# One decoder block on one core: GpSimd adds up the two parts of h, bucket copies split, small reorderings at the start and before the output projection

## The reference, cut to what matters

```python
def reference(x, attn_norm_g, w_in, ...):          # 512 tokens, 1024 channels, float32
    h = rmsnorm(x, attn_norm_g[l])
    proj = h @ w_in[l]
    u_b, u_c, u_x, q, k, v, g_conv, g_attn = jnp.split(proj, SPLITS, axis=-1)
    y_conv = (u_b * short_conv(u_c * u_x, conv_w[l])) @ w_conv_out[l]
    attn = sliding_window_attention(q, k, v, attn_sinks[l], rel_bias)   # 16 heads, 2 KV heads, window 128
    mixed = sigmoid(g_conv) * y_conv + sigmoid(g_attn) * (attn @ w_attn_out[l])
    x = x + mixed @ w_o[l]
    h2 = rmsnorm(x, mlp_norm_g[l])
    x = x + square(relu(h2 @ w_up[l])) @ w_down[l]
    return rmsnorm(x, final_norm_g)
```

## Time and profile before

| | |
|---|---|
| time, median of 3 runs | 752.34 us (752.04 to 752.34) |
| the profiled execution's own time | 752.0 us |
| its span in the trace | 750.3 us |
| PE busy | 740.4 us (99%), 4201 matmuls |
| DVE busy | 656.4 us (87%) |
| ACT busy | 429.7 us (57%) |
| POOL busy | 85.2 us (11%) |
| DMA | 135.45 MB, mean 181 GB/s |
| granted PE clock | 0.9 or more in all 40 slices |

### The profile page before, as it was taken

One profiled execution on the slowest core, in us unless ns is written; L12 is line 12 of the kernel. 1 busy time (PEld: TensorE's weight loads), 2 busy tenths in 40 slices (PEclk: granted clock), 3 DMA queues, 4 the chain that ended last, 5 costly groups with the idle time before them and its releaser, 6 DMA issues.

```text
span 750.3 us, 10666 instructions
## 1 busy us (share of the span) xinstructions
PE 740.4 (99%) x4201; PEld 650.1 (87%) x4201; DVE 656.4 (87%) x759; ACT 429.7 (57%) x548; POOL 85.2 (11%) x120
## 2 busy tenths in 40 slices
PE   8999999999999999999999999999999999999996
PEld 8899888888888888888878899889988999899985
DVE  6995888889899686989999999998799879986997
ACT  6773555453644557564658776654465455545555
POOL 1520000111122101010100101010101010100102
PEclk9999999999999999999999999999999999999999
DMA  9999313162247987778766747777677668676703
GB/s 324 188 309 333 113 56 114 57 159 66 84 125 232 310 232 193 199 224 200 248 169 168 217 125 209 181 196 197 169 186 203 176 170 220 168 212 182 196 0 114
DMA packets 69443, 135.45 MB, mean 181 GB/s; under 512 B 2636, under 2 KB 18068, under 8 KB 69396
## 3 DMA queue, kind: packets, MB, share of 16 engines
q1 hardware_dynamic: 48848, 85.23, 33.9%
q0 software_dynamic: 20336, 49.30, 30.6%
q10 hardware_dynamic: 212, 0.28, 0.1%
HBM read 128.48 MB, written 6.32 MB: 180 GB/s over the span
## 4 chain that ended last, share of the span: by engine, by line
PE 94%; DMA 3%; DVE 1%; ACT 1%; issue 0%; DVEq 0%; ACTq 0%
PE pair L1086 45%; PE pair L1045 21%; PE pair L790 6%; PE pair L792 6%; PE pair L791 6%; PE pair L912 4%; DMA q_raw<-in_w_in 3%; PE pair L837 2%; PE pair L812 1%; PE pair L811 1%; PE pair L821 1%; PE pair L1008 0%; DMA xn<-in_x 0%; PE pair L996 0%; PE pair L851 0%
## 5 line engine op out<-in xcount | busy, mean ns | idle before, releaser
L1386 ACT ACTIVATE high<-home_raw 128x2048 fp32r<-128x2048 f32 x91 | 174.4, 1916 | 148.8 <-PE pair L1086 103.4
L2005 DVE TENSOR_TENSOR home_lo<-home_raw,high 128x2048 fp32r<-128x2048 f32 x91 | 208.4, 2291 | 34.0 <-ACT high L1386 33.6
L1086 PE MATMUL pair<-high,s_hi_tile 128*128 128x512 f32 x440 | 110.3, 391 | 0.7 <-ACT pair L1571 0.7
L1086 PE MATMUL pair<-high,s_lo_tile 128*128 128x512 f32 x440 | 109.9, 390 | 0.0
L1086 PE MATMUL pair<-home_lo,s_hi_tile 128*128 128x512 f32 x440 | 109.5, 389 | 0.0
L1086 PEld LDWEIGHTS pair<-high,s_hi_tile 128*128 128x128 f32 x440 | 81.8, 188 | 18.1 <-issue 1.1
L1086 PEld LDWEIGHTS pair<-home_lo,s_hi_tile 128*128 128x128 f32 x440 | 82.5, 188 | 17.1
L1086 PEld LDWEIGHTS pair<-high,s_lo_tile 128*128 128x128 f32 x440 | 82.5, 188 | 17.0
L790 PE MATMUL pair<-h,wgt 128*128 128x512 f32 x192 | 76.5, 399 | 0.0
L792 PE MATMUL pair<-h,wgt 128*128 128x512 f32 x192 | 75.0, 390 | 0.0
L791 PE MATMUL pair<-h,wgt 128*128 128x512 f32 x192 | 74.9, 390 | 0.0
(11 more groups left out here) (227 smaller groups left out, 1127.5 us busy)
## 6 DMA issues: line engine op xcount, KB each, us to landing
home_raw<-in_w_up SPq DMA_DIRECT2D x16, 1024.0 KB, 5.4
home_raw<-in_w_down SPq DMA_DIRECT2D x16, 1024.0 KB, 5.0
raw<-in_w_in SPq DMA_DIRECT2D x26, 512.0 KB, 4.8
home_raw<-in_w_up POOLq DMA_DIRECT2D x12, 1024.0 KB, 8.3
home_raw<-in_w_down POOLq DMA_DIRECT2D x12, 1024.0 KB, 8.5
home_raw<-in_w_in POOLq DMA_DIRECT2D x7, 1024.0 KB, 8.6
home_raw<-in_w_in SPq DMA_DIRECT2D x7, 1024.0 KB, 6.7
home_raw<-in_w_conv_out SPq DMA_DIRECT2D x4, 1024.0 KB, 5.2
```

Source lines behind the costliest of these rows:

```text
L1086: last = mm(pair[region(s, i)][:, b, :], a_[:, k, b * P:(b + 1) * P], w[:, k, :], start=(fresh and kind == 0 and k == 0), stop=(kind == 2 ...
L1386: a(high[n % 2][:, :], home_raw[home_of(s, name)][:, :], ACT.Copy).then_inc(m_hi, 1)
L2005: v.tensor_tensor(home_lo[home][:, :], home_raw[home][:, :], f32(high[n % 2][:, :]), ALU.subtract).then_inc(m_lo, 1)
```

## The change

POOL adds high and low part of the first token half of h into a new tile `h_whole`, in two instructions of 128 x 1024 elements (`first_whole`): the first between `add_q(M7)` and the bucket copies, the second between `add_q(M5)` and the first store. The three sums of h that use the first token half then take DVE one operation each. Of the 32 bucket copies, 14 stay where they were and 18 move behind `add_q(N4)`. `h_s1` moves ahead of `q_sum_t2`. ACT writes the second token half so that the first four tiles are whole before the last two are begun. The high parts of M1's weights are made in quarters, those of M5's in halves (and M5's kind 0 goes by k). At the start, the gains are transposed and copied before the second block of x is waited for, and 3 idle transposes fewer are made. In stage WO the first half of the seed copy stands before `s_high(WO, N2)`.

```diff
-        hs_part = place("hs_part", [P, 4, 2 * P], offset=hs_at[0])
+        h_whole = place("h_whole", [P, KT, 2 * P], offset=one[3])
...
+            def first_whole(j):
+                u = h_whole[:, 4 * j:4 * j + 4, :]
+                g.tensor_tensor(u, f32(four_of(h[:, 0, :, :], 0, j)), f32(four_of(h[:, 1, :, :], 0, j)), ALU.add
+                                ).then_inc(h_added, 1)
+            def buckets(first, end):
...
             add_q(M7, 1, 1, q_t3_in)
+            pool.wait_ge(h_ready, 8)
+            first_whole(0)
             pool.wait_ge(table_in, 16 * 2)
             pool.wait_ge(ext_step, 1)
...
+            buckets(0, 14)
...
+            first_whole(1)
             store_sum(M6)
             pool.wait_ge(q_low, 5)
             add_q(N4, 1, 0, q_t4_in)
+            buckets(14, BUCKETS)
             store_sum(M5)
...
-            idle_transposes(28)
-            x_transposes(0)
+            idle_transposes(25)
             pe.wait_ge(rows_in, 16 * 3)
             nc.tensor.transpose(bank[KT - 1][:, T - 5 * KT:T], prow[:, :], ident[0:5 * KT, 0:5 * KT]).then_inc(par_t, 1)
+            x_transposes(0)
             x_transposes(1)
...
-                        by_k = i == M6 and kind == 0
+                        by_k = i in (M6, M5) and kind == 0
...
+                n = 512 if i == M1 else 1024
+                for c0 in range(1024 * e, 1024 * e + 1024, n):
+                    a(q_hi[Q_ORDER.index(i) % 2][:, cols(c0, n)], q_raw[i][:, cols(c0, n)], ACT.Copy).then_inc(q_high, 1)
+
+            def q_high_t1(e):
+
+                act.wait_ge(q_t1_in, 16)
+                act.wait_ge(q_prod, 2 * Q_ORDER.index(N2) + 2)
                 c = cols(1024 * e, 1024)
-                a(q_hi[Q_ORDER.index(i) % 2][:, c], q_raw[i][:, c], ACT.Copy).then_inc(q_high, 1)
+                a(q_hi[1][:, c], q_raw[M5][:, c], ACT.Copy).then_inc(q_high, 1)
...
+            tile_whole(0, 0)
+            tile_whole(1, 4)
...
+            for k in (1, 5, 2, 3, 6, 7):
+                tile_whole(LATE_TILES.index(k), k)
...
             sum_high(M6)
+            sum_high(M5)
             q_high_t2()
-            sum_high(M5)
-            q_high_part(M5)
+            q_high_t1(0)
+            q_high_t1(1)
...
+            seed_out(0)
             s_high(WO, N2)
...
+            seed_out(1)
...
             scale_x(0)
-            scale_x(1)
             dve.wait_ge(par_t, 1)
             v.tensor_copy(pcol[:, :], bank[KT - 1][:, T - 5 * KT:T]).then_inc(par_ready, 1)
+            scale_x(1)
...
             def h_s3():
 
+                dve.wait_ge(wide, 6)
+                dve.wait_ge(h_added, 1)
+                v.tensor_tensor(hs_sum[0][:, :, :], h_whole[:, 0:4, :], four_of(qa, 1, 0), ALU.subtract).then_inc(hs_step, 1)
...
             h_s3()
             h_s2()
+            h_s1()
             q_sum_t2()
             sum_low(M6)
-            h_s1()
             q_low_part(M6)
```

More of the change, by code:

```diff
@@ L364, in build @@
         h_hi, h_ready = sem("h_hi"), sem("h_ready")
-        wide = sem("wide")
+        wide, h_added = sem("wide"), sem("h_added")
         q_b11, q_b21 = ([sem(f"{n}{e}") for e in range(2)] for n in ("q_b11_", "q_b21_"))
@@ L675, in add_q @@
                                accum_op=ALU.add).then_inc(done, 16)
+            def first_whole(j):
[3 more added lines that the diff above has]
+            def buckets(first, end):
+                bucket = t5_bucket(np.arange(WINDOW))
+                for b in range(first, end):
+                    dist = np.flatnonzero(bucket == b)
+                    m0, n = 2 * P - 1 - int(dist[-1]), len(dist)
+                    g.tensor_copy(ext[:, m0:m0 + n], rbt[:, b:b + 1].to_broadcast([HEADS, n])).then_inc(ext_step, 1)
             g.memset(ext[:, :], NEG).then_inc(ext_step, 1)
@@ L889, in q_product @@
                         if kind == 0:
-                            pe.wait_ge(q_high, 5 if i == M6 else at_ + 4)
+                            pe.wait_ge(q_high, {M6: 7, M5: 9}.get(i, at_ + 7))
                         elif kind == 2:
@@ L899, in q_product @@
                     for k, f in order:
-                        if i == M6 and kind == 0 and (k, f) == (2, 0):
-                            pe.wait_ge(q_high, 6)
+                        if i in (M6, M5) and kind == 0 and (k, f) == (2, 0):
+                            pe.wait_ge(q_high, {M6: 8, M5: 10}[i])
                         if early_ and k + 1 > seen:
@@ L1246, in q_high_part @@
                 at_ = Q_ORDER.index(i)
-                act.wait_ge({M5: q_t1_in, M7: q_t3_in, M3: q_b22, N4: q_t4_in}[i], 16)
+                act.wait_ge({M7: q_t3_in, M3: q_b22, N4: q_t4_in}[i], 16)
                 act.wait_ge(q_prod, 2 * (at_ - 2) + 2)
@@ L1268, in late_high @@
                     tile_high(1, at_, LATE_TILES[at_])
-            def late_whole(n):
-                for at_ in (2 * n, 2 * n + 1):
-                    tile_whole(at_, LATE_TILES[at_])
             root(0)
@@ L1306, in q_copy @@
                 if i:
-                    act.wait_ge(hs_step, 3)
+                    act.wait_ge(hs_step, 2)
                 a(four_of(qa, i, j), four(Q_REGION.get(of, 3))[:, :, :], ACT.Copy, scale=scale).then_inc(done, 1)
@@ L1566, in _, with seed_out @@
             mixed_copy(2)
+            def seed_out(b):
+                act.wait_ge(prod, 14 * WO + 2 * M1 + b + 1)
+                act.wait_ge(mix_ready, 3)
+                a(pair[region(WO, N2)][:, b, :], pair[region(WO, M1)][:, b, :], ACT.Copy).then_inc(o_seeded, 1)
+            seed_out(0)
             s_high(WO, N2)
[L1568 to L1571, removed]
+            seed_out(1)
             high_part(WO, M6)
@@ L1750, in q_low_half @@
                 at_, c = Q_ORDER.index(i), cols(1024 * e, 1024)
-                dve.wait_ge(q_high, 2 * at_ + e + 1)
+                dve.wait_ge(q_high, 2 * e + 2 if i == M1 else 4 + e + 1)
                 v.tensor_tensor(q_lo[i][:, c], q_raw[i][:, c], f32(q_hi[at_ % 2][:, c]), ALU.subtract).then_inc(q_low, 1)
@@ L1756, in q_low_part @@
                 at_ = Q_ORDER.index(i)
-                dve.wait_ge(q_high, at_ + 4)
+                dve.wait_ge(q_high, {M6: 8, M5: 10}.get(i, at_ + 7))
                 if i == M6:
@@ L1809, in _ @@
             late_low(3)
-            def h_part(part, i, j):
-                return f32(four_of(h[:, part, :, :], i, j))
             def step_done(n):
@@ L1817, in h_s3, with h_s2 @@
             def h_s3():
-                dve.wait_ge(wide, 8)
[L1820 to L1825, removed]
+                dve.wait_ge(wide, 6)
+                dve.wait_ge(h_added, 1)
+                v.tensor_tensor(hs_sum[0][:, :, :], h_whole[:, 0:4, :], four_of(qa, 1, 0), ALU.subtract).then_inc(hs_step, 1)
+            def h_s2():
+                step_done(1)
+                dve.wait_ge(wide, 8)
                 v.scalar_tensor_tensor(out=hs_sum[1][:, :, :], in0=four_of(qa, 1, 1), scalar=-1.0, in1=hs_sum[0][:, :, :],
@@ L1829, in h_s1 @@
             def h_s1():
[L1830 to L1833, removed]
+                step_done(2)
+                v.tensor_tensor(hs_sum[2][:, :, :], h_whole[:, 0:4, :], hs_sum[1][:, :, :], ALU.add).then_inc(hs_step, 1)
             def h_s4():
[L1836 to L1839, removed]
+                step_done(2)
+                dve.wait_ge(h_added, 2)
+                v.tensor_tensor(hs_sum[3][:, :, :], h_whole[:, 4:8, :], hs_sum[1][:, :, :], ALU.add).then_inc(hs_step, 1)
             def sum_low(i):
```

9 lines of the change are left out of this document (2 added, 7 removed).

## The result

The changed kernel takes 766.66 us (median of 6 runs, 764.21 to 767.89) against 752.34 (6 runs, 751.92 to 752.88): ratio 1.0187, 95% interval 1.0177 to 1.0197, 14.3 us slower. The forecast was 761.5, the upper end of its range 764.5. The profiled execution took 766.6 with a span of 764.9, 14.6 over the span of before.

What follows compares the result with a forecast made beforehand. PE was taken to bound the kernel, busy 740.4 of 750.3 us. From the profiled 752.0: - 0.1 (start) + 8.6 (M3 late) + 1.5 (slow restart) - 0.5 (stage WO) = 761.5 us, range 753.0 to 764.5.

Steps and rivals of the forecast that it cites:

- Start: Kernel start up to M1: gain's copy into DVE idle time, quarters for halves; -0.1 us, bounds +0.5 and -0.2.
- First POOL addition: Kv strip: addition runs 20.35 to 22.7 after DVE's subtractions and delays a weight split; +1.4 us, 0 to 1.8.
- Second addition: Sums of h: takes the port at 31.5 after DVE's sums, ends 33.8; M6 starts at 36.0.
- The 18 copies: Behind `add_q(N4)`: start at 40.2, about 9 at once, then one per DVE seam, last ending about 49.3.
- bias_rows: SP's store after the copies, ahead of M3's load: 3.0 us from issue to landing, of 2.2 to 3.8.
- M3's weights: Load issued at 52.3 instead of 39.00, 6.1 us of 4.8 to 7.5, landed at 58.4; M3 starts at 61.5.
- PE after the pause: M3 after 7.7 us idle on PE: slow restart costs +1.5 us, of 0 to 2.2.
- Stage WO: Seed's first half ahead of ACT's high part of N2 shortens PE's wait: -0.5 us, of 0 to -0.7.
- No holding up: Rival: POOL's additions run beside DVE without stopping it, only gains remain; 750.4 us, chance 0.16.
- the copies fit: Rival: all 18 moved copies done at the first opening, by 42.5, no long pause before M3; 753.5 us, chance 0.18.
- long additions: Rival: a POOL addition takes 5.3 us with the port held, delaying strip and copies; 766 us, chance 0.08.

Runs made afterwards that it cites:

- seed_only: The kernel before, with only the seed's first half copied ahead of ACT's high part of N2 in stage WO: 752.27 us, ratio 0.9998.
- first_add_alone: The kernel before plus POOL's first addition alone, after `add_q(M7)` and ahead of all 32 bucket copies, result unused: 755.33 us, ratio 1.0039.
- copies_only: As four_steps, but 18 of the 32 bucket copies stand behind `add_q(N4)`: 763.05 us, ratio 1.0126.
- stores_later: The changed kernel with POOL's stores of the sums of M5, M7 and M3 held until M3's weights have landed: 761.94 us, ratio 1.0118.
- add_in_gap: The changed kernel without the second addition, the first behind copy 20 and DVE's second kv-strip weight split, all copies ahead of `add_q(M5)`: 761.83 us, ratio 1.0122.
- adds_only: The changed kernel with all 32 bucket copies in their old place, both POOL additions kept: 755.82 us, ratio 1.0045.
- load_first: The changed kernel, but SP issues M3's weights before it waits for the bucket copies and stores the bias rows: 757.19 us, ratio 1.0055.
- four_steps: The changed kernel without POOL's additions (DVE's sums with two operations, old order) and all bucket copies in their old place: 751.25 us, ratio 0.9984.
- pe_kept_busy: The changed kernel with 96 transposes of unused result on PE in the pause ahead of M3: 766.34 us, ratio 1.0179.

## Why the prediction was wrong in size

The direction, the largest term and its whole chain were right; the time lies 2.2 us above the range. From the forecast, 9.5 over the profiled execution of before, to the measured 14.6:

- *Start, -0.1.* M1 starts at 9.61, 0.1 later than before (9.52). No gain shows; with the old start M1 began anywhere from 9.41 (`seed_only`) to 9.87 (`first_add_alone`), so a tenth can't be told.
- *First POOL addition, +1.4 on the strip.* **This step failed.** It said that the addition waits for DVE's subtractions until 20.35 and then delays a weight split, and it gave 1.8 as the bound for an earlier start. The addition came in between the two halves, the second half ended 3.0 late, and alone the addition cost 2.9 (`first_add_alone`). Its length was right: 2.35 forecast, 2.40 where nothing contends. The bound had both waits in it, for the low part and for a split; it was sized too small. In the changed kernel they are 1.17 and 0.70, and the clock fell behind them (last section).
- *Second addition.* **Failed in its order**, too: I had it wait for all three sums of DVE; it held up the first. From the start of `h_s3` to the end of the third sum 7.2 passed, not 6.0, and that start was 1.5 late already. M6 started at 38.95, not 36.0, and its low part ended at 42.25, not 39.4. PE was ready for M3 at 56.75 instead of 53.8, which by itself was hidden in the pause; what counted is that the copies shifted with it.
- *The 18 copies* behaved as written, one to a seam: 8.6 from the first one's start, 9.1 forecast. They ended at 51.95, not 49.3: +2.65. By the two steps above the first copy came 3.1 late (43.34, not 40.2), and the copies took 0.5 less.
- *bias_rows:* 1.54, under the bound of 2.2: -1.45. This was luck, and hid a part of the next error. In `copies_only` the store took 3.7 and the load behind it 7.6; the two together took 11.3 there and 11.0 here, where 9.1 were forecast.
- *M3's weights, 6.1 of 4.8 to 7.5:* 9.46. **The second step that failed**, +3.35. The stores of M5's and M7's sums were named as neighbours, but no row gave them a price, and the upper bound of 7.5 was too low. `stores_later` shows 5.3 without them: they are 4.2 of the 9.5. With 3.0 instead of 3.1 for ACT's two operations, M3 starts 2.65 - 1.45 + 3.35 - 0.1 = 4.5 later than 61.5.
- *PE after the pause, +1.5 of 0 to 2.2:* 1.9. The row that spoke for 0 was no ground for it: it shows a granted clock of 1.00 over transposes that went at half the later pace, so it did not explain even its own stretch. Here the clock did fall, while PE stood idle. The Trainium skill, TensorE: Matmul & The Clock Gate, Part 1, says that an idle TensorE falls to the 1.2 GHz level, and the trace agrees (0.52 in the slice from 60, 0.50 from 62 to 70).
- *Stage WO, -0.5:* about -0.4 by the wait (0.3 left of 0.7).
- *The rivals.* "No holding up" is refuted by DVE's 5.22 and 4.68, "the copies fit" by 8.6 us of copies, "long additions" by 2.40. The 766 of that last rival is near the measured time by chance; its mechanism did not occur.

Added up: 4.5 at M3, 0.4 in the pause, 0.1 in stage WO and 0.1 at the start are the 5.1 between 9.5 and 14.6. The large errors share a cause: where something ran beside something else, the bounds were too narrow on the slow side (1.8 against 2.9 for the addition, 7.5 against 9.46 for the load).

## What to carry to other kernels

A short instruction on a lightly used engine costs what stands behind it in its queue: 18 copies of 0.13 us each cost 11.8 us here, 12 copies in `add_in_gap` about 10, because in a dense stretch of DVE only a copy or two gets in between two instructions, and the issue of a load stood behind the last copy. Before moving POOL work, find which loads are issued behind it, also through another queue's wait, and place it beside DVE operations that read PSUM. And when a transfer becomes critical, count the bytes that are issued just ahead of it on the other queues: moving the stores of the sums behind the load of M3's weights was worth about 4.7 us (766.66 against 761.94, the latter with a wide spread).

## What the runs showed of the hardware that was not expected

*Who gets the port.* The rows of an addition overlap the DMA issue ahead of it. From the end of the issue to the end of the addition it is 2.44 (first) and 2.42 us (second; also 2.42 in `adds_only` and 2.37 in `load_first` for the first), the 2.40 of a free addition. DVE instructions that started at least a tenth of a microsecond after that issue began were held to the addition's end: N2's second half; `h_s3` (29.36, issue at 29.23); in `adds_only` already the first half (18.39, issue at 17.72). Those that began before it or right with it were not: N2's first half (18.20, issue at 18.55), and in `adds_only` the scaling of x (17.73, issue at 17.72), which took the usual 0.75. In `load_first` the scaling of a block of x, which reads one tile and a factor per row, started 0.11 after the issue (17.62) and was held:

```profile
17.73 4.15 DVE L1768 TENSOR_SCALAR xn<-xn,rms 128x1024 f32<-128x1024 f32 x1
```

An issue with no addition behind it holds nothing up (in `four_steps` the issue runs from 29.42 to 30.71, and the two weight sums of DVE from 30.40 took 2.35, as usual). Why a waiting addition should hold the port already is open; that the victim changes with the landing of one load, by a few tenths, goes with what PE then waited for it: 0.96, 1.17 and 1.31 for a low part in `first_add_alone`, the changed kernel and `adds_only`, 3.25 for x in `load_first`.

*The clock after shorter waits.* After waits of 1.17 and 0.70 close together, the granted clock in the slices 26 to 28 and 28 to 30 was 0.50 and 0.66 in the changed kernel, and 1.00 in `first_add_alone` with 0.96 and 0.70. It was also 1.00 in `stores_later` and `pe_kept_busy`, which are the changed kernel up to there, with 1.31 and 0.70. What decides this no run shows. The strip's matmuls stood 0.43 apart instead of 0.227 there. It cost little, since M6's operands came late anyway: in `adds_only`, with the clock at 1.00 there, M6 started at 39.13.
